# Layer 0's latent tiles as one, one and two instead of one and three, with new numbers of loop slots per unit

## The chip, the cores and the metric

The kernel runs on one core of one Trainium2 chip. The metric is the device time of one execution in microseconds (us). The kernel before takes 4186.02 us, the median of 3 runs (4184.7 to 4189.01).

## The reference, cut to what matters

Five tiles of 128 tokens (one prompt tile, four latent tiles) pass through two layers. Layer 0 is a mixer (chunked GLA heads beside pooling groups), layer 1 windowed attention; after either comes an output projection and then PEER, a layer of 16384 experts of which each token reads 128 (8 heads, 16 each):

```python
qh = (x @ w_q).reshape(T, PEER_HEADS, 2, PEER_HALF)
s = jnp.einsum('thcd,hcnd->thcn', qh, keys)
...                                   # top 16 of each half, top 16 of the pair sums
act = jax.nn.gelu(jnp.einsum('thkd,td->thk', u[eb], xb))
return jnp.einsum('thk,thkd->td', (gb * act).astype(xb.dtype), v[eb])
```

Everything is float32. For one tile and one of its 128 experts a row of u and of v (8 KB together) is fetched for each of the 128 tokens: 1.05 MB. There are 5 tiles, 2 layers and 128 experts, so 1280 such fetches.

## The kernel before, in words

**Two programs in one.** The first is the sequence of stages (norm, projection, GLA, pooling, output and norm, queries, selection, attention) on TensorE, VectorE and ScalarE. The second is the expert loop of class `Experts`, called the loop here. It is cut into 1280 slots, one for each fetch. For a slot GpSimd issues an indirect DMA into one of 8 ring buffers (L1889), VectorE makes the dot product of the u rows with the tile's hidden rows (L1906), ScalarE makes the weight (L1929, L1932) and either a diagonal matrix for TensorE (L1935), which adds the v rows (L1946), or nothing, and VectorE adds them (L1921). GpSimd's queue holds nothing but the fetches, in order, each waiting for its ring buffer, and at the start of a tile for that tile's selection. After a tile's 128 slots VectorE ends the tile (L1959 to L1963): it adds the sums to x. That is called a turn here.

**What sets the order.** The slots are written in between the instructions of the stages. Every stage has a number of units and a triple (slots per unit, ring places that TensorE adds, slots written at the stage's start, its lead); `PE_6` gives TensorE six of the eight places and VectorE two, `PE_8` all eight, and `PE_0` stands for none but the first and the last slot of a tile. After unit u the loop is brought up to slot `base + int(u * rate)` on each engine (`Stage.tick`), and at the stage's end to `base + int(units * rate)` (`Stage.__exit__`). `bg.allow(n)` sets the limit: no slot from n * 128 on is written until the call. A selection has 21 units by the count but ticks after 17 of them, so what belongs to the last 4 is written behind it. Every stage ends in a meeting of four engines (L153 to L168), and the tag of a stage is in its tiles' names.

**Layer 0.** The prompt tile goes first, without the loop. Then latent tile 1 alone goes through GLA, pooling, output, queries and selection as unit s0a while the loop works on the prompt tile's slots; latent tiles 2, 3 and 4 go through the same five stages together as unit s0b (their selections one by one). Output and queries stream their weights for each unit anew: `w_out` in 4 chunks, `peer_wq` in 16, the keys once, on SyncE's queue. Then come the modulation of layer 1 (`mod1`), `bg.finish(2)`, which runs the loop up to slot 384 and ends that tile if the loop isn't past it, and a meeting. If the loop is past slot 384 by then, `finish` only brings it to at least slot 388, which is nothing where it is past that too.

**Layer 1.** The prompt and latent tiles 1 and 2 go together (unit j1), with two selections, `j1_select0` under the limit 640 and `j1_select1` under 768; then tile 2 of attention as s1b and tiles 3 and 4 as s1c. After the last selection the loop runs alone up to slot 1280.

The slot that the loop has reached at the end of each stage, by the arithmetic above:

| stage | units | lead | per unit | slot at the end |
|---|---|---|---|---|
| s0a_query | 16 | 2 | 1.0 | 65 |
| s0a_select | 21 | 3 | 0.8 | 84 |
| s0b_gla, three tiles | 24 | 4 | 2.0 | 136 |
| s0b_pool | 3 | 4 | 2.0 | 146 |
| s0b_out | 18 | 3 | 1.75 | 180 |
| s0b_query | 16 | 2 | 2.0 | 214 |
| s0b_select2, 3, 4 | 21 each | 3 | 1.5, 2.1, 2.1 | 248, 295, 342 |
| mod1 | 12 | 3 | 2.5 | 375 |
| finish(2) | | | | 384 |
| j1_norm | 3 | 5 | 3.0 | 398 |
| j1_query | 16 | 2 | 1.0 | 582 |
| j1_select0, j1_select1 | 21 each | 3 | 2.0, 2.1 | 627, 674 |
| s1b_query, s1b_select | 16, 21 | 2, 3 | 1.15, 2.1 | 796, 843 |
| s1c_out, s1c_query | 12, 16 | 3, 2 | 1.9, 1.15 | 943, 963 |
| s1c_select3, s1c_select4 | 21 each | 3 | 2.0, 2.1 | 1008, 1055 |

## Time and profile before

| | us |
|---|---|
| median of 3 runs | 4186.02 |
| the profiled execution's own time | 4198.27 |
| its span in the trace | 4196.5 |
| TensorE busy | 2963.8 (71%) |
| VectorE busy | 3050.2 (73%) |
| ScalarE busy | 1414.7 (34%) |
| GpSimd busy | 1608.1 (38%) |

The profiled execution's time is 1.77 us over its span, and 12.25 us over the median. The DMA engines moved 1521.91 MB, a mean of 363 GB/s. The expert loop starts at 391 us, the last selection ends at 3615.5 us, and from there on only the loop runs. A stage's limits are read from the drains of its closing meeting; the windows shown further down are cut at these limits, one for each stage, and give for each engine the busy time with the number of instructions in brackets.

### The profile page before, as it was taken

To read this page: it belongs to the slowest core of one execution; us is meant where nothing else is said; L and a number is where in the kernel's file an instruction comes from. 1 tells how busy PE (TensorE), PEld (TensorE's weight loads), DVE (VectorE), ACT (ScalarE), POOL (GpSimd) and SP (SyncE) were. 2 spreads that over 40 slices of the span, in tenths; PEclk is the share of its full clock that TensorE was granted. 3 is DMA by queue.
4 is the path that set the end of the run, shared out by engine and by line. 5 is a ranking of instruction groups with operands and counts; after the bars stand their busy time and mean duration, and the time that the engine had idled before them with its cause. 6 is when DMAs were issued, how large, how long until landed. Compare 5 with 4: busy or idle time off the path is not lost.

```text
span 4196.5 us, 32629 instructions
## 1 busy us (share of the span) xinstructions
PE 2963.8 (71%) x9247; PEld 1533.7 (37%) x9247; DVE 3050.2 (73%) x6149; ACT 1414.7 (34%) x4109; POOL 1608.1 (38%) x1311
## 2 busy tenths in 40 slices
PE   5699756875877744857768776776877687665666
PEld 1365442444522311423446323444354543222222
DVE  0405769878897846697878876878787898666666
ACT  1212423532233312235522332432454233322222
POOL 0000332434544424344443443434433454454554
PEclk7798887987999976877879987878988899888888
DMA  7243897889998999899999999999999999999998
GB/s 305 110 156 114 311 407 288 332 339 362 417 397 360 396 407 390 339 391 407 374 383 390 417 374 365 364 379 417 395 372 391 414 406 380 423 420 409 415 421 369
DMA packets 222322, 1521.91 MB, mean 363 GB/s; under 512 B 29757, under 2 KB 33537, under 8 KB 48822
## 3 DMA queue, kind: packets, MB, share of 16 engines
q0 software_dynamic: 187200, 1370.25, 80.8%
q1 hardware_dynamic: 34942, 149.58, 9.0%
q8 instruction: 74, 1.21, 0.1%
q14 instruction: 106, 0.87, 0.1%
HBM read 1516.49 MB, written 3.24 MB: 362 GB/s over the span
## 4 chain that ended last, share of the span: by engine, by line
DMA 31%; PE 29%; DVE 24%; issue 7%; ACT 4%; POOL 2%; DVEq 1%; SPq 1%; PEldq 1%; PEld 0%; POOLq 0%; ACTq 0%
DMA core_ring<-in_l_uv,core_experts 27%; PE sum_rows L1946 7%; DVE core_ring L1906 7%; DVE core_yv L1921 5%; PE sum_rows L2213 2%; POOL core_ring L1889 2%; PE j_in_ps L471 2%; PE s1b_in_ps L471 1%; DMA s0a_h_w<-in_l_peer_wq 1%; PE s1c_query_pq L1679 1%; PE j_query_pq L1679 1%; DMA mod_w<-in_l_w_mod 1%; DVEq L158 1%; PE p_in_ps L471 1%; PE s0b_out_po L610 1%
## 5 line engine op out<-in xcount | busy, mean ns | idle before, releaser
L1889 POOL DMA_INDIRECT core_ring<-in_l_uv,core_experts x1280 | 1593.4, 1245 | 2233.3 <-PE sum_rows L1946 1104.6
L1946 PE MATMUL sum_rows<-core_ring,core_diag 128*128 128x512 f32 x3004 | 1646.0, 695 | 639.3 <-ACT core_diag L1935 506.5
L1906 DVE CUSTOM_DVE_ANT_0 core_ring<-core_ring,core_hc 128x1024 f32<-128x1024 f32 x1280 | 1552.2, 1223 | 659.7 <-DMA core_ring<-in_l_uv,core_experts 475.2
L1946 PEld LDWEIGHTS sum_rows<-core_ring,core_diag 128*128 128x128 f32 x3004 | 617.7, 219 | 1590.3 <-ACT core_diag L1935 848.9
L1929 ACT ACTIVATE core_wt<-core_wt 128x1 f32<-128x1 f32 x1280 | 256.5, 200 | 1681.3 <-DVE core_wt L1906 1589.4
L1921 DVE SCALAR_TENSOR_TENSOR core_yv<-core_ring,core_wt,core_yv 128x1024 f32<-128x1024 f32 x519 | 665.3, 1282 | 19.1 <-ACT core_wt L1932 18.6
L1932 ACT ACTIVATE core_wt<-core_wt,core_gates 128x1 f32<-128x1 f32 x1280 | 376.8, 294 | 41.5
L1935 ACT ACTIVATE core_diag<-core_ident,core_wt 128x128 f32<-128x128 f32 x751 | 301.5, 401 | 24.5
L2213 PE MATMUL sum_rows<-core_ring 128*128 128x416 f32 x320 | 117.6, 527 | 5.2 <-DVEq L158 4.1
L1929 ACT ACT_TABLE_LOAD x81 | 103.9, 1283 | 5.2 <-DVEq L158 3.8
L1906 DVE DVE_READ_ACCUMULATOR2_ANT core_wt<- 128x1 f32 x1280 | 105.6, 83 | 0.0
L1679 PE MATMUL s0b_query_pq<-s0b_h_hT,s0b_h_w 128*128 128x384 f32 x256 | 85.1, 497 | 5.4 <-DVEq L158 5.4
L2213 PEld LDWEIGHTS sum_rows<-core_ring 128*128 128x128 f32 x320 | 61.9, 196 | 57.0 <-issue 56.8
L2146 POOL DMA_DIRECT2D core_ring<-in_l_w_in x5 | 2.7, 535 | 205.4 <-PE sum_rows L2213 205.4
L357 PE MATMUL mod_pm<-mod_w,mod_c_silu 128*32 128x512 f32 x192 | 45.0, 944 | 38.6 <-DMA mod_w<-in_l_w_mod 38.6
L471 PE MATMUL j_in_ps<-j_in_w,j_atth_hT 128*128 128x384 f32 x192 | 64.8, 503 | 6.0 <-DMA j_in_w<-in_l_w_in 6.0
L1679 PE MATMUL j_query_pq<-s_att_pr,j_h_w 128*128 128x256 f32 x256 | 59.7, 393 | 8.8 <-DVEq L158 7.8
L1679 PEld LDWEIGHTS s0b_query_pq<-s0b_h_hT,s0b_h_w 128*128 128x128 f32 x256 | 49.7, 195 | 40.6 <-issue 8.0
L1679 PE MATMUL s1c_query_pq<-s1c_h_hT,s1c_h_w 128*128 128x256 f32 x256 | 57.4, 389 | 5.4 <-DVEq L158 5.4
L610 PE MATMUL s0b_out_po<-s0b_h_w,s0b_h_hT 128*128 128x256 f32 x192 | 49.4, 422 | 11.1 <-ACT s0b_h_hT L633 6.5
L1679 PEld LDWEIGHTS j_query_pq<-s_att_pr,j_h_w 128*128 128x128 f32 x256 | 49.7, 197 | 18.8 <-issue 8.2
L1598 ACT ACT_TABLE_LOAD x40 | 51.3, 1283 | 13.6 <-DVE s1c_attend_mx L1625 5.1
(772 smaller groups left out, 3060.2 us busy)
## 6 DMA issues: line engine op xcount, KB each, us to landing
mod_w<-in_l_w_mod SPq DMA_DIRECT2D x16, 2048.0 KB, 12.7
core_ring<-in_l_uv,core_experts POOLq DMA_INDIRECT x1280, 10.4
core_ring<-in_l_w_mod POOLq DMA_DIRECT2D x8, 2048.0 KB, 10.7
p_in_w<-in_l_w_in SPq DMA_DIRECT2D x5, 1664.0 KB, 9.1
core_ring<-in_l_w_in POOLq DMA_DIRECT2D x5, 1664.0 KB, 10.5
p_h_w<-in_l_peer_wq SPq DMA_DIRECT2D x16, 512.0 KB, 4.6
s0a_h_w<-in_l_peer_wq SPq DMA_DIRECT2D x16, 512.0 KB, 12.9
s0b_h_w<-in_l_peer_wq SPq DMA_DIRECT2D x16, 512.0 KB, 8.1
```

Of the source, the lines that this page charges most:

```text
L471: mm = nc.tensor.matmul(ps[:, i % 4, 0:chunk], hT[:, k, t * P:(t + 1) * P], w[:, n % 2, k, :], start=(k == 0), stop=(k == DK - 1))
L610: mm = nc.tensor.matmul(po[:, t % 2, n * CH:(n + 1) * CH], own(t)[:, k, :], w[n % w_slots][:, k * CH:(k + 1) * CH], start=(k == 0), stop=( ...
L1598: nc.scalar.activation(sc[:, n % 2, 0:w], sc[:, n % 2, 0:w], ACT.Exp, bias=mx[:, n % 2:n % 2 + 1], accum_out=den[:, t % 2, head:head + 1]) ...
L1679: mm = nc.tensor.matmul(pq[:, n % 2, 0:tok], queries.chunk(n)[:, k, :], hT[:, k, :], start=(k == 0), stop=(k == DK - 1))
L1889: nc.gpsimd.indirect_dma_start(self.ring[:, r, :], None, core.a[f"l{layer}_uv"], bass.IndirectOffsetOnAxis(ap=self.experts[:, t, n:n + 1], ...
L1906: nc.vector.tensor_tensor_reduce(self.ring[:, r, 0:D], self.ring[:, r, 0:D], self.hc[:], 1.0, 0.0, ALU.mult, ALU.add, self.wt[:, r:r + 1]) ...
L1921: x = nc.vector.scalar_tensor_tensor(self.yv[:], self.ring[:, r, D:], self.wt[:, r:r + 1], self.yv[:], ALU.mult, ALU.add)
L1929: nc.scalar.activation(self.wt[:, r:r + 1], self.wt[:, r:r + 1], ACT.Gelu_apprx_tanh).then_inc(self.gelu_done, 1)
L1932: nc.scalar.activation(self.wt[:, r:r + 1], self.wt[:, r:r + 1], ACT.Copy, scale=gate).then_inc(self.wt_done, 1)
L1935: nc.scalar.activation(self.diag[:, r, :], self.core.env["ident"][:], ACT.Copy, scale=self.wt[:, r:r + 1]).then_inc(self.diag_done, 1)
L1946: mm = nc.tensor.matmul(self.py[:, c * 512:(c + 1) * 512], self.diag[:, r, :], self.ring[:, r, D + c * 512:D + (c + 1) * 512], start=(at = ...
L2213: mm = nc.tensor.matmul(self.ps[:, i % 2 * 512:i % 2 * 512 + self.CH], self.hT[:, k, t * P:(t + 1) * P], w[:, k, :], start=(k == 0), stop= ...
```

## The change

Latent tiles 2, 3 and 4 no longer go as one unit. Tile 2 goes alone as unit s0b, in the way of tile 1: GLA and pooling for this tile, then `first_experts` with two weight buffers and the hidden rows of tile 3 as room for the transposed rows, under the limit 256. Tiles 3 and 4 follow as unit s0c, under the limit 384 and then as before. The numbers per unit are set anew.

```diff
--- before.py
+++ after.py
@@ -2357,9 +2357,10 @@
 PROMPT_RATES = {"norm": (3.0, PE_4, 5), "in": (2.0, PE_0, 4), "qk": (0.625, PE_4, 5), "attend": (2.25, PE_5, 3), "out": (1.5, PE_0, 4),
                 "query": (0.6, PE_0, 2), "select": (2.1, PE_8, 3)}
 FIRST_RATES = {"norm": (2.0, PE_4, 5), "decay": (2.0, PE_8, 0), "gla": (1.6, PE_6, 4), "pool": (2.0, PE_2, 4),
-               "out": (1.7, PE_0, 3), "query": (1.0, PE_0, 2), "select": (0.8, PE_8, 3)}
-REST_RATES = {"norm": (3.0, PE_4, 5), "gla": (2.0, PE_6, 4), "pool": (2.0, PE_2, 4), "out": (1.75, PE_0, 3), "query": (2.0, PE_0, 2),
-              "first select": (1.5, PE_8, 3), "select": (2.1, PE_8, 3)}
+               "out": (1.7, PE_0, 3), "query": (1.0, PE_0, 2), "select": (1.1, PE_8, 3)}
+SECOND_RATES = {"gla": (2.0, PE_6, 4), "pool": (2.0, PE_2, 4), "out": (1.9, PE_0, 3), "query": (1.15, PE_0, 2), "select": (1.8, PE_8, 3)}
+REST_RATES = {"gla": (2.0, PE_6, 4), "pool": (2.0, PE_2, 4), "out": (1.9, PE_0, 3), "query": (1.25, PE_0, 2),
+              "first select": (2.0, PE_8, 3), "select": (2.1, PE_8, 3)}
 LATENT_RATES = {"norm": (3.0, PE_4, 5), "in": (1.4, PE_0, 4), "qk": (1.125, PE_4, 5), "attend": (2.25, PE_5, 3), "out": (1.9, PE_0, 3),
                 "query": (1.15, PE_0, 2), "first select": (2.0, PE_8, 3), "select": (2.1, PE_8, 3)}
 
@@ -2408,8 +2409,11 @@
             layer0_mix(core, "s0a", latents, [0], pr, la, st, constants, (BAND_FIRST, BAND_AFTER), FIRST_RATES)
             first_experts(core, "s0a", first, 0, FIRST_RATES, None, 2, env["h"][:, others[0], :])
             bg.allow(2)
-            layer0_mix(core, "s0b", latents, [1, 2, 3], pr, la, st, constants, (BAND_AFTER, BAND_BEFORE), REST_RATES)
-        other_experts(core, "s0b", latents[1:], 0, 1, REST_RATES)
+            layer0_mix(core, "s0b", latents, [1], pr, la, st, constants, (BAND_AFTER, BAND_BEFORE), SECOND_RATES)
+            first_experts(core, "s0b", latents[1], 0, SECOND_RATES, None, 2, env["h"][:, latents[2], :])
+            bg.allow(3)
+            layer0_mix(core, "s0c", latents, [2, 3], pr, la, st, constants, (BAND_AFTER, BAND_BEFORE), REST_RATES)
+        other_experts(core, "s0c", latents[2:], 0, 2, REST_RATES)
         with Stage(core, "mod1_c") as m:
             modulation_stage(core, 1, "mod1", m.sb("silu", [P, DK, 32])[:], early.MOD_CHUNKS, [1, 4], 2, (2.5, PE_0, 3))
         with Stage(core, "s1_att") as m:
```
The slots at the ends of the stages are now:

| stage | units | lead | per unit | slot at the end |
|---|---|---|---|---|
| s0a_select | 21 | 3 | 1.1 | 91 |
| s0b_gla, one tile | 8 | 4 | 2.0 | 111 |
| s0b_pool | 1 | 4 | 2.0 | 117 |
| s0b_out | 6 | 3 | 1.9 | 131 |
| s0b_query | 16 | 2 | 1.15 | 151 |
| s0b_select | 21 | 3 | 1.8 | 191 |
| s0c_gla, two tiles | 16 | 4 | 2.0 | 227 |
| s0c_pool | 2 | 4 | 2.0 | 235 |
| s0c_out | 12 | 3 | 1.9 | 260 |
| s0c_query | 16 | 2 | 1.25 | 282 |
| s0c_select3, s0c_select4 | 21 each | 3 | 2.0, 2.1 | 327, 374 |
| mod1 | 12 | 3 | 2.5 | 407 |
| finish(2) | | | | 407 (writes nothing) |
| j1_norm | 3 | 5 | 3.0 | 421 |
| j1_query | 16 | 2 | 1.0 | 605 |
| j1_select0, j1_select1 | 21 each | 3 | 2.0, 2.1 | 640 (the limit), 687 |
| s1c_select4 | 21 | 3 | 2.1 | 1068 |

**SyncE's queue.** These rows are the loads of the output and query stages of unit s0b before; `h_w` is the weights' buffer, `room` holds the queries and the keys.

```order
L568 DMA s0b_h_w<-in_l_w_out 128x2048
L574 DMA s0bq_room<-mods 3x1024
L568 DMA s0b_h_w<-in_l_w_out 128x2048 x3
L519 DMA s0bq_room<-in_l_peer_keys 128x2048
L520 DMA s0bq_room<-in_k_count 128x32
L508 DMA s0b_h_w<-in_l_peer_wq 128x1024 x8
L166 UNCONDITIONAL_BRANCH
L171 ISA x16
L1666 UNCONDITIONAL_BRANCH
L508 DMA s0b_h_w<-in_l_peer_wq 128x1024 x8
```

And of the changed kernel, first unit s0b, then unit s0c:

```order
L568 DMA s0b_h_w<-in_l_w_out 128x2048
L574 DMA s0bq_room<-mods 3x1024
L568 DMA s0b_h_w<-in_l_w_out 128x2048 x3
L508 DMA s0b_h_w<-in_l_peer_wq 128x1024 x4
L519 DMA s0bq_room<-in_l_peer_keys 128x2048
L520 DMA s0bq_room<-in_k_count 128x32
L166 UNCONDITIONAL_BRANCH
L171 ISA x14
L1666 UNCONDITIONAL_BRANCH
L508 DMA s0b_h_w<-in_l_peer_wq 128x1024 x12
```

```order
L568 DMA s0c_h_w<-in_l_w_out 128x2048
L574 DMA s0cq_room<-mods 3x1024
L568 DMA s0c_h_w<-in_l_w_out 128x2048 x3
L519 DMA s0cq_room<-in_l_peer_keys 128x2048
L520 DMA s0cq_room<-in_k_count 128x32
L508 DMA s0c_h_w<-in_l_peer_wq 128x1024 x8
L166 UNCONDITIONAL_BRANCH
L171 ISA x16
L1666 UNCONDITIONAL_BRANCH
L508 DMA s0c_h_w<-in_l_peer_wq 128x1024 x8
```

`w_out`, the keys and the 16 chunks of `peer_wq` are loaded twice; with two buffers 4 query chunks go in the output stage and 12 in the query stage, with four buffers 8 and 8. The pooling constants (1.5 MB, ahead of each unit's GLA) are loaded once more too.

**VectorE around finish(2).** These rows stand ahead of the meeting before layer 1's norm (L156 is the meeting, L1906 the dot product, L1899 takes the next tile's hidden rows):

```order
L1921 SCALAR_TENSOR_TENSOR core_yv<-core_ring,core_wt,core_yv 128x1024
L1959 TENSOR_TENSOR core_yv<-core_yv,sum_rows 128x1024
L1961 TENSOR_TENSOR core_yv<-core_yv,core_g 128x1024
L1963 TENSOR_TENSOR core_x<-core_x,core_yv 128x1024
L156 UNCONDITIONAL_BRANCH
L2020 UNCONDITIONAL_BRANCH
L1899 COPY core_hc<-core_h 128x1024
```

In the changed kernel, from the last sums of `mod1` on (L320):

```order
L320 TENSOR_TENSOR mod_m<-mod_m,mod_ps 2x512 x2
L2020 UNCONDITIONAL_BRANCH
L156 UNCONDITIONAL_BRANCH
L2020 UNCONDITIONAL_BRANCH
L1906 ISA core_ring,core_wt<-core_ring,core_hc 128x1024
L1906 ISA core_wt 128x1
L1921 SCALAR_TENSOR_TENSOR core_yv<-core_ring,core_wt,core_yv 128x1024
```

The slots 375 to 383 and the end of the tile (L1959 to L1963) no longer stand between the modulation and the meeting; they stand in `mod1`, and the loop crosses the meeting in the middle of a tile.

**VectorE at the end of j1_select0.** Before, from the last wide reduction of the selection (L1808) on:

```order
L1808 TENSOR_REDUCE j_select_ef<-j_select_rest 128x128
L1906 ISA core_ring,core_wt<-core_ring,core_hc 128x1024
L1906 ISA core_wt 128x1
L1906 ISA core_ring,core_wt<-core_ring,core_hc 128x1024
L1906 ISA core_wt 128x1
L1810 SCALAR_TENSOR_TENSOR core_experts<-j_select_ef 128x128
L1813 TENSOR_REDUCE j_select_gs<-j_select_ts 128x8
L1814 RECIPROCAL j_select_gs<-j_select_gs 128x8
L1816 TENSOR_TENSOR core_gates<-j_select_ts,j_select_gs 128x128
L2020 UNCONDITIONAL_BRANCH
L1906 ISA core_ring,core_wt<-core_ring,core_hc 128x1024
L1906 ISA core_wt 128x1
```

After the change:

```order
L1808 TENSOR_REDUCE j_select_ef<-j_select_rest 128x128
L1810 SCALAR_TENSOR_TENSOR core_experts<-j_select_ef 128x128
L1813 TENSOR_REDUCE j_select_gs<-j_select_ts 128x8
L1814 RECIPROCAL j_select_gs<-j_select_gs 128x8
L1816 TENSOR_TENSOR core_gates<-j_select_ts,j_select_gs 128x128
L2020 UNCONDITIONAL_BRANCH x2
L1899 COPY core_hc<-core_h 128x1024
L1906 ISA core_ring,core_wt<-core_ring,core_hc 128x1024
L1906 ISA core_wt 128x1
L1906 ISA core_ring,core_wt<-core_ring,core_hc 128x1024
```

Before, ten slots stand behind L1808, two of them ahead of the four small operations that close the selection and eight behind them. After it none does, since the loop has reached the limit of 640 slots; the next one is the first slot of the tile that this selection chooses experts for.

## Rows read from the trace of the kernel before

**Rows 1.** The page: DMA queue of the gathers; the chain that ended last.
```profile
q0 software_dynamic: 187200, 1370.25, 80.8%
...
DMA 31%; PE 29%; DVE 24%; issue 7%; ACT 4%; POOL 2%; DVEq 1%; SPq 1%; PEldq 1%; PEld 0%; POOLq 0%; ACTq 0%
```

**Rows 2.** Windows, one per stage from s0a_select to j1_norm; the first row names the columns.
```profile
core 0: us, PE busy (x) PEld busy (x) DVE busy (x) ACT busy (x) POOL busy (x), PEclk, DMA share, GB/s
633.30:704.10 70.80, 46.66 (x96) 19.28 (x96) 69.14 (x258) 19.55 (x59) 21.61 (x18) 0.77 0.80 308
704.40:888.90 184.50, 146.25 (x696) 73.24 (x696) 164.26 (x280) 89.95 (x201) 64.69 (x53) 0.91 0.81 303
888.90:915.30 26.40, 19.89 (x104) 13.94 (x104) 20.76 (x29) 8.92 (x27) 12.52 (x10) 0.89 0.87 343
915.30:1038.80 123.50, 69.82 (x256) 53.64 (x256) 95.22 (x119) 30.67 (x86) 51.27 (x35) 0.73 0.95 377
1038.80:1133.50 94.70, 85.11 (x256) 49.71 (x256) 81.67 (x102) 23.06 (x84) 51.47 (x35) 0.95 1.01 408
1133.50:1222.40 88.90, 67.59 (x156) 29.39 (x156) 86.50 (x288) 33.04 (x104) 42.87 (x33) 0.93 0.98 396
1222.40:1355.10 132.70, 93.89 (x216) 38.15 (x216) 105.52 (x317) 44.70 (x143) 56.00 (x49) 0.92 0.90 372
1355.10:1478.50 123.40, 94.39 (x220) 39.14 (x220) 100.06 (x312) 45.10 (x144) 53.85 (x47) 0.96 0.99 399
1478.80:1633.30 154.50, 62.27 (x228) 13.87 (x228) 87.13 (x117) 25.63 (x82) 57.91 (x34) 0.65 0.97 395
1633.30:1663.10 29.80, 15.43 (x24) 5.27 (x24) 20.49 (x26) 7.38 (x26) 12.79 (x11) 0.79 1.00 400
1663.10:1712.90 49.80, 31.82 (x60) 13.89 (x60) 31.37 (x43) 21.26 (x48) 11.56 (x11) 0.64 0.62 244
```

**Rows 3.** Windows of other stages of the same kinds, and of the closing stretch.
```profile
438.40:504.20 65.80, 48.04 (x228) 23.89 (x228) 52.11 (x89) 27.73 (x62) 17.47 (x17) 0.87 0.87 329
519.50:573.90 54.40, 32.56 (x96) 21.43 (x96) 36.00 (x46) 14.84 (x36) 18.80 (x14) 0.72 0.98 400
573.90:633.30 59.40, 34.52 (x256) 32.05 (x256) 43.32 (x54) 11.75 (x52) 20.57 (x18) 0.95 1.02 417
2259.30:2371.40 112.10, 88.99 (x200) 38.32 (x200) 99.97 (x310) 42.92 (x137) 55.93 (x45) 0.93 0.99 394
2371.40:2501.60 130.20, 97.08 (x216) 39.86 (x216) 105.29 (x317) 44.71 (x143) 55.84 (x47) 0.91 0.93 380
2832.10:2895.20 63.10, 35.49 (x256) 33.67 (x256) 48.39 (x60) 12.80 (x56) 25.66 (x20) 0.85 1.02 417
2895.20:3013.80 118.60, 93.10 (x208) 38.81 (x208) 102.60 (x314) 44.70 (x143) 57.59 (x48) 0.93 1.01 417
3229.90:3316.20 86.30, 50.11 (x180) 36.15 (x180) 67.89 (x86) 23.22 (x64) 36.24 (x25) 0.76 1.02 419
3316.20:3376.50 60.30, 57.44 (x256) 49.99 (x256) 48.00 (x60) 14.30 (x56) 23.43 (x20) 0.97 1.01 411
3376.50:3487.40 110.90, 87.88 (x200) 35.84 (x200) 99.73 (x310) 42.92 (x137) 56.33 (x45) 0.94 0.99 407
3487.40:3615.50 128.10, 96.04 (x216) 39.98 (x216) 104.94 (x317) 44.71 (x143) 54.78 (x47) 0.91 0.95 387
3615.80:4196.50 580.70, 361.63 (x576) 127.37 (x576) 385.35 (x541) 169.31 (x594) 276.96 (x220) 0.82 0.99 408
```

**Rows 4.** The page's groups of instructions: the two VectorE operations of a slot.
```profile
L1906 DVE CUSTOM_DVE_ANT_0 core_ring<-core_ring,core_hc 128x1024 f32<-128x1024 f32 x1280 | 1552.2, 1223 | 659.7 <-DMA core_ring<-in_l_uv,core_experts 475.2
...
L1921 DVE SCALAR_TENSOR_TENSOR core_yv<-core_ring,core_wt,core_yv 128x1024 f32<-128x1024 f32 x519 | 665.3, 1282 | 19.1 <-ACT core_wt L1932 18.6
```

**Rows 5.** DMA issues between 704 and 1663 us: the weights of unit s0b.
```profile
s0b_h_w<-in_l_peer_wq SPq DMA_DIRECT2D x16, 512.0 KB, 8.1
...
s0b_h_w<-in_l_w_out SPq DMA_DIRECT2D x4, 1024.0 KB, 17.0
```

## The prediction

> **What bounds the kernel now.** I read the page first: the queue of the gathers alone takes 80.8% of the sixteen DMA engines' time, and the chain that ended last is led by its landings, 27% [rows 1]. The second view is one window per stage. In the closing stretch, where nothing but the loop runs, 225 slots (1055 to 1280) take 580.7 us at a DMA share of 0.99: 2.58 us a slot [rows 3]. That is the pace of the DMA engines, and the coin of this prediction: a slot that the loop does earlier takes 2.58 us from the end, and a stage that loads weights beside the loop pays in the same coin. In the stages from s0a_query on the share is 0.90 to 1.02 nearly everywhere; idle are s0a_select (0.80, VectorE busy 69.14 of 70.8 us), s0b_gla (0.81, VectorE 164.26 of 184.5 us) and j1_norm (0.62) [rows 2]. So only the first of these can be filled by writing more slots into it.
>
> A third thing to see is the price of a turn. Four selections of 47 slots with the same rate: j1_select1 and s1c_select4 hold a turn and take 130.2 and 128.1 us at a share of 0.93 and 0.95; s1b_select and s0b_select4 hold none and take 118.6 and 123.4 us [rows 2, 3]. The difference of the means, 8.2 us, is idle DMA time behind a turn.
>
> **The change part by part**, in us against the profiled execution, slots from the two tables.
>
> s0a_select goes from 19 to 26 slots. All of them are summed by TensorE there, so VectorE, which ends this stage, gets 7 dot products of 1.22 us [rows 4]: +8.5. At the loop's pace it would be 18.1, the upper bound; the lower is 6.8, as VectorE has 1.7 us free.
>
> GLA was 184.5 us for three tiles and 52 slots. The nearest row for one tile is s0a_gla, 65.8 us with 16 slots [rows 3]; 4 slots more at 1.22 + 1.28 / 4 (VectorE adds two of eight, [rows 4]) make 72.0. Two tiles are 72.0 + (184.5 - 8.2 - 72.0) / 2 = 124.2, with the turn at slot 128 taken out, since it moves to s0b_query. Together 196.2: +11.7. Bounds +2.4 (the 4 slots free) and +21.9 (4 at 2.58, and the turn no saving).
>
> Pooling was 26.4 us for 10 slots [rows 2]; 14 slots at the same 2.64 us are 37.0: +10.6 (at the loop's pace 4 slots are 10.3, so the ends lie close).
>
> The output stage: one tile with 14 slots is s0a_out, 54.4 us with 13, plus one slot, 57.0; two tiles with 25 slots are s1c_out, 86.3 us [rows 3]. Together 143.3 against 123.5 [rows 2]: +19.8. The turn at 256 now lies in it; weight loads can fill its gap, so between 0 and 8.2, and I take half, 4.1. Sum +23.9.
>
> The queries: one tile with 20 slots is s0a_query, 59.4 us with 18, plus two slots, 64.6 (s1b_query, with the same 20 slots, took 63.1); two tiles with 22 slots are s1c_query, 60.3 us with 20, plus two, 65.5 [rows 3]. Together 130.1 against 94.7 [rows 2]: +35.4, and half of a turn for slot 128: +39.5. This is the largest term, and it is the second reading of the weights: the old stage did 34 slots with one pass over `peer_wq`, the new ones 42 with two.
>
> What is read again is 12288 KB of the two weights [rows 5] and 2588 KB of keys, rows and pooling constants (shapes of the queue's rows), 15.2 MB. s0a_query moved 417 GB/s at a share of 1.02 [rows 3]; at this rate it is 36.5 us if no idle time takes any of it.
>
> The selections: 88.9 + 132.7 + 123.4 = 345.0 us for 128 slots [rows 2]. After: 40 slots at the pace of s1b_select (118.6 / 47 = 2.52), 100.8; 45 slots as s1c_select3, 110.9; 47 as the mean without a turn, 121.0 [rows 3]. s1c_select3 moved 110.9 us x 407 GB/s = 45.1 MB, two slots less than it used, so 5 us of it had been fetched ahead, and I add them: 337.7, -7.3. The lower bound is -12.3. VectorE doesn't end s0b_select: of its 86.50 us in s0b_select2, 34 dot products are 41.6, so the selection is 44.9, and with 40 slots it is 93.9, under 100.8.
>
> mod1 keeps its 33 slots and gets the turn at 384: half of one, +4.1.
>
> finish(2), 29.8 us for 9 slots and the end of the tile at a share of 1.00 [rows 2], goes but for the meeting: -29.5. What is late next is j1_norm. Its 14 slots went with 11 gathers issued, since the meeting had found the ring full [rows 2]; now the ring is empty at the meeting: 3 slots less two that its idle share can still take up to 7.7 us, I take 6.0. Bounds 0 and 7.7.
>
> Layer 1 runs as before with the loop 23 slots ahead, until j1_select0 meets the limit of 640: 35 slots instead of 45 there. The two selections of j1 lose 10 slots, -25.8. In return GpSimd has no fetch to issue until the selection is complete: the last reduction, four small operations, then a fetch that lands from an idle queue. I price it as a second turn, +8.2 (bounds 0 and 16.4): -17.6.
>
> The closing stretch has 212 slots instead of 225: -33.5.
>
> Sum: 8.5 + 11.7 + 10.6 + 23.9 + 39.5 - 7.3 + 4.1 - 29.5 + 6.0 - 17.6 - 33.5 = +16.4. The profiled execution took 4198.27 us, 12.25 over the median of the runs; a difference of this size carries over, so 4186.0 + 16.4 = 4202.4. In short: 36.5 us of loads, of which 20 find DMA time that was idle, in s0a_select and behind turns.
>
> **A rule of the skill.** In s0a_query 12 chunks of weights came on SyncE's queue beside GpSimd's gathers, and 18 slots took 59.4 us, 3.30 each instead of 2.58, at a share of 1.02 [rows 3]. The Trainium skill says it so (DMA: Bandwidth & Descriptors, "Issuing engines are not separate DMA queues"): DMAs of whatever engine run on the same 16 DMA engines and interleave. It speaks against this change, and read strictly it gives the first rival below; the trace agrees where the share is 1.02, and leaves room where it is 0.80. The skill's HBM Reference (Specifications) gives some 358 GB/s a core; by that the estimate for 15.2 MB would be 42.5 us, but the row has 417 GB/s, and the measurement decides.
>
> **The rivals.** First, full price: the reloads cost 36.5 us and no idle time is reclaimed, because what s0a_select takes up is lost again in front of the limit at 640 and in the additional start and end of a GLA stage. For it: GLA at 0.81, which the change doesn't touch and splits into two prologues [rows 2]. Against it: the selection's turn is surely gone. 4222.5.
>
> Second, the other side, faster: every turn that the change moves hides. The turns at 128, 256 and 384 move from stages without loads into s0b_query, s0c_out and mod1, which have weights to fetch whatever the ring does. If the loads fill the gap whole, and likewise the wait at 640 costs nothing since the selection would have to end anyway, all low bounds hold together: 8.5 + 2.4 + 10.6 + 19.8 + 35.4 - 12.3 + 0 - 29.5 + 0 - 25.8 - 33.5 = -24.4, so 4161.6. It decides for faster once a moved turn costs under 1 us in its new stage and GLA's two parts stay under 190 us together. Against it: mod1 at 0.97 and s0c_out's model at 1.02 have no slack, so a gap of 8 us there has nothing to be filled with but what the stage loads anyway [rows 2, 3].
>
> Third, the wait at 640 is dear: the fetch queue stands from the last fetch of the old tile until a landing, and the usual turn follows at once, each at 8.2 plus the lost cover of about 10 us: +26 to +28 in all, 4213.
>
> Fourth, the change does nothing that can be told: the gain of 13 slots and of finish (63 us) and the price of the split cancel closer than I have it. Within 0.2% of the median, 8.4 us, is about what a measurement of this kernel can tell from no change.
>
> **How the numbers follow.** The forecast (4194 to 4211) has 0.45, full price 0.20, dear wait 0.07, cancelling 0.14, faster 0.14. Of the forecast's own part some 0.06 lies inside 0.2%. Faster by over 0.2%: 0.15; within: 0.21; slower: 0.64. The range of 8 in 10 reaches down half of the way to the second rival and up past the first: 4177 to 4227; the forecast's own is 4194 to 4211.
>
> **What would show it.** In the windows of the changed kernel: s0b_query near 65 us and s0c_query near 66 at a share of 1.0 with 20 and 22 slots; s0b_out 57, s0c_out 86 to 94; s0a_select near 79 with VectorE over 0.95; the two GLA stages 72 and 124; no stretch of its own for finish; j1_select0 near 90 with an idle DMA gap at its end; the closing stretch 547. The bytes moved go from 1521.91 to about 1537 MB. The forecast is wrong if the four output and query stages stay under 250 us together, or if the closing stretch is not shorter by 33 us.

## The result

The changed kernel takes 4202.2 us, the median of 5 runs (4194.54 to 4210.25); the kernel before took 4186.02 us (4180.56 to 4189.01) beside it. The ratio is 1.0041, with a 95% interval from 1.0027 to 1.0055: slower by 0.27 to 0.55%. A second measurement on another chip gave 1.0031 [1.0017, 1.0046]. The forecast was 4202 us, with a range from 4177 to 4227.

**The profile after.** The profiled execution took 4194.54 us, the lowest of its five, while that of before lay 12.25 us over its median. So the two traces alone differ by -3.8 us where the medians differ by +16.2, and a sum over stages must be read with a second trace of the changed kernel beside it (4219.41 us, the highest of its ten). The page's rows that answer to [rows 1]:

```profile
q0 software_dynamic: 187200, 1370.25, 80.6%
q1 hardware_dynamic: 38932, 164.81, 9.9%
...
DMA 31%; PE 27%; DVE 25%; issue 8%; ACT 3%; POOL 2%; DVEq 1%; SPq 1%; PEldq 1%; PEld 0%; POOLq 0%; ACTq 0%
```

The gathers are the same bytes; SyncE's queue carries 15.2 MB more than the 149.58 MB and 9.0% of before. The two shares together are 90.5% of 4192.7 us, 3794 us of DMA time, against 89.8% of 4196.5 us, 3768 us; in the second trace 90.2% of 4217.6 us, 3804 us. So the DMA engines work 26 and 36 us longer and stand idle 30 and 15 us less (398 and 413 us instead of 428). Each share is printed to 0.1%, so each of these times is good to some 4 us. The mean, 22 us of idle time taken up, is near the forecast's 20 (of 36.5 us of loads).

Windows of the changed kernel, one per stage, with the columns of [rows 2]: s0a_select; GLA, pooling, output, queries and selection of s0b; the same of s0c with its two selections; mod1; the meeting in finish's place; j1_norm; j1_select0 and j1_select1; the closing stretch.

```profile
629.30:707.90 78.60, 55.23 (x124) 21.34 (x124) 77.16 (x272) 25.84 (x80) 30.60 (x25) 0.87 0.90 350
708.20:772.00 63.80, 52.05 (x244) 25.98 (x244) 57.80 (x98) 31.07 (x73) 25.36 (x22) 0.97 0.99 391
772.00:789.20 17.20, 10.72 (x44) 6.64 (x44) 11.24 (x16) 5.74 (x17) 6.28 (x5) 0.80 0.77 299
789.20:845.00 55.80, 32.64 (x100) 21.47 (x100) 35.31 (x47) 16.14 (x40) 18.63 (x13) 0.73 0.93 373
845.00:914.20 69.20, 41.33 (x260) 36.38 (x260) 51.40 (x63) 13.26 (x56) 24.38 (x21) 0.83 0.94 383
914.20:1014.80 100.60, 78.43 (x180) 33.97 (x180) 93.53 (x300) 38.42 (x122) 51.16 (x41) 0.92 1.01 415
1015.10:1141.50 126.40, 105.28 (x472) 52.42 (x472) 108.98 (x187) 60.27 (x137) 40.71 (x37) 0.88 0.89 342
1141.50:1164.10 22.60, 16.66 (x72) 10.42 (x72) 15.32 (x22) 7.21 (x22) 7.93 (x7) 0.87 0.78 287
1164.10:1258.20 94.10, 51.74 (x180) 36.58 (x180) 70.42 (x89) 23.91 (x66) 34.99 (x24) 0.74 0.97 389
1258.20:1321.10 62.90, 56.22 (x256) 49.06 (x256) 52.93 (x66) 15.86 (x60) 31.87 (x23) 0.96 0.98 402
1321.10:1433.20 112.10, 88.19 (x200) 37.90 (x200) 99.83 (x310) 42.92 (x137) 53.83 (x45) 0.92 1.01 416
1433.20:1554.70 121.50, 93.22 (x220) 38.62 (x220) 100.15 (x312) 45.11 (x144) 54.41 (x47) 0.97 0.99 404
1555.00:1710.50 155.50, 64.14 (x236) 15.15 (x236) 88.43 (x119) 26.43 (x84) 64.50 (x34) 0.66 0.97 396
1710.50:1714.90 4.40, 0.00 (x0) 0.00 (x0) 0.00 (x0) 0.00 (x0) 0.00 (x0) 0.50 1.00 411
1714.90:1773.90 59.00, 35.38 (x64) 15.89 (x64) 33.58 (x44) 22.16 (x51) 14.34 (x12) 0.63 0.57 222
2322.70:2413.80 91.10, 69.78 (x160) 29.68 (x160) 87.52 (x290) 33.94 (x107) 38.70 (x30) 0.91 0.90 353
2413.80:2542.20 128.40, 95.81 (x216) 39.55 (x216) 105.03 (x317) 44.71 (x143) 60.95 (x52) 0.90 0.96 395
3647.90:4192.70 544.80, 336.52 (x544) 117.54 (x544) 363.18 (x510) 159.65 (x560) 258.47 (x207) 0.82 0.99 410
```

Beside the second trace, term by term, in us against the trace of before (worked out from unrounded limits, so a tenth can differ from the rows above):

| term | forecast | after | second trace |
|---|---|---|---|
| s0a_select | +8.5 | +7.8 | +7.8 |
| GLA | +11.7 | +5.7 | +11.9 |
| pooling | +10.6 | +13.4 | +14.8 |
| output | +23.9 | +26.3 | +29.6 |
| queries | +39.5 | +37.5 | +38.4 |
| three selections | -7.3 | -10.7 | -9.0 |
| mod1 | +4.1 | +0.9 | +0.9 |
| finish | -29.5 | -25.4 | -25.5 |
| j1_norm | +6.0 | +9.2 | +15.0 |
| j1's selections | -17.6 | -22.8 | -24.2 |
| closing stretch | -33.5 | -35.9 | -35.0 |
| sum | +16.4 | +6.0 | +24.7 |

The mean of the two sums is +15.4. That it lies so near the medians' +16.2 says little, since there is only one trace of the kernel before. Stages that the change doesn't touch differ between the first two traces by some -10 us together; I take that for the spread of single executions (the ten times of the changed kernel on the second chip span 26.6 us).

### The profile page after: what moved, and what is told of

Read it like the earlier page. It is cut to its first block, busy times and chain, and to the rows that moved or that the text cites. A ratio compares the mean times of both kernels' runs of the same rounds, so it can differ in the third digit from the quotient of the medians.

```text
span 4192.7 us, 33299 instructions
## 1 busy us (share of the span) xinstructions
PE 2957.0 (71%) x9507; PEld 1564.2 (37%) x9507; DVE 3050.0 (73%) x6153; ACT 1420.3 (34%) x4128; POOL 1609.9 (38%) x1311
## 3 DMA queue, kind: packets, MB, share of 16 engines
q8 instruction: 76, 1.25, 0.1%
## 4 chain that ended last, share of the span: by engine, by line
DMA 31%; PE 27%; DVE 25%; issue 8%; ACT 3%; POOL 2%; DVEq 1%; SPq 1%; PEldq 1%; PEld 0%; POOLq 0%; ACTq 0%
DMA core_ring<-in_l_uv,core_experts 25%; PE sum_rows L1946 7%; DVE core_ring L1906 7%; DVE core_yv L1921 5%; PE sum_rows L2213 2%; POOL core_ring L1889 2%; PE j_in_ps L471 2%; PE s1c_query_pq L1679 1%; DVEq L158 1%; PE j_query_pq L1679 1%; DMA mod_w<-in_l_w_mod 1%; PE s1b_in_ps L471 1%; PE p_in_ps L471 1%; PE p_query_pq L1679 1%; PE j_out_po L610 1%
## 5 line engine op out<-in xcount | busy, mean ns | idle before, releaser
L1946 PE MATMUL sum_rows<-core_ring,core_diag 128*128 128x512 f32 x2996 | 1625.4, 690 | 604.6 <-ACT core_diag L1935 462.2
L1906 DVE CUSTOM_DVE_ANT_0 core_ring<-core_ring,core_hc 128x1024 f32<-128x1024 f32 x1280 | 1549.8, 1223 | 662.4 <-DMA core_ring<-in_l_uv,core_experts 435.9
L1946 PEld LDWEIGHTS sum_rows<-core_ring,core_diag 128*128 128x128 f32 x2996 | 613.3, 218 | 1538.1 <-ACT core_diag L1935 798.5
L1921 DVE SCALAR_TENSOR_TENSOR core_yv<-core_ring,core_wt,core_yv 128x1024 f32<-128x1024 f32 x521 | 667.1, 1280 | 19.1 <-ACT core_wt L1932 18.8
L1929 ACT ACT_TABLE_LOAD x82 | 105.2, 1283 | 7.1 <-DVEq L158 5.7
L1906 DVE DVE_READ_ACCUMULATOR2_ANT core_wt<- 128x1 f32 x1280 | 104.6, 82 | 0.0
L471 PE MATMUL j_in_ps<-j_in_w,j_atth_hT 128*128 128x384 f32 x192 | 63.8, 496 | 9.6 <-DMA j_in_w<-in_l_w_in 9.6
L357 PE MATMUL mod_pm<-mod_w,mod_c_silu 128*32 128x512 f32 x192 | 40.0, 865 | 36.4 <-DMA mod_w<-in_l_w_mod 36.4
L1679 PEld LDWEIGHTS j_query_pq<-s_att_pr,j_h_w 128*128 128x128 f32 x256 | 49.2, 196 | 19.7 <-issue 8.2
L1679 PE MATMUL s0c_query_pq<-s0c_h_hT,s0c_h_w 128*128 128x256 f32 x256 | 56.2, 383 | 0.4 <-PEq L163 0.4
L1598 ACT ACT_TABLE_LOAD x40 | 51.3, 1283 | 15.1 <-DVE s1a_attend_mx L1625 4.4
L1679 PEld LDWEIGHTS s1c_query_pq<-s1c_h_hT,s1c_h_w 128*128 128x128 f32 x256 | 50.0, 196 | 13.0 <-issue 5.8
L1679 PE MATMUL s0a_query_pq<-core_h,s0a_h_w 128*128 128x128 f32 x256 | 39.0, 318 | 21.0 <-DMA s0a_h_w<-in_l_peer_wq 17.9
## 6 DMA issues: line engine op xcount, KB each, us to landing
mod_w<-in_l_w_mod SPq DMA_DIRECT2D x16, 2048.0 KB, 12.5
core_ring<-in_l_uv,core_experts POOLq DMA_INDIRECT x1280, 10.5
core_ring<-in_l_w_in POOLq DMA_DIRECT2D x5, 1664.0 KB, 10.7
s0a_h_w<-in_l_peer_wq SPq DMA_DIRECT2D x16, 512.0 KB, 12.5
```

The lines of the kernel that those rows point to most:

```text
L471: mm = nc.tensor.matmul(ps[:, i % 4, 0:chunk], hT[:, k, t * P:(t + 1) * P], w[:, n % 2, k, :], start=(k == 0), stop=(k == DK - 1))
L1598: nc.scalar.activation(sc[:, n % 2, 0:w], sc[:, n % 2, 0:w], ACT.Exp, bias=mx[:, n % 2:n % 2 + 1], accum_out=den[:, t % 2, head:head + 1]) ...
L1679: mm = nc.tensor.matmul(pq[:, n % 2, 0:tok], queries.chunk(n)[:, k, :], hT[:, k, :], start=(k == 0), stop=(k == DK - 1))
L1906: nc.vector.tensor_tensor_reduce(self.ring[:, r, 0:D], self.ring[:, r, 0:D], self.hc[:], 1.0, 0.0, ALU.mult, ALU.add, self.wt[:, r:r + 1]) ...
L1921: x = nc.vector.scalar_tensor_tensor(self.yv[:], self.ring[:, r, D:], self.wt[:, r:r + 1], self.yv[:], ALU.mult, ALU.add)
L1929: nc.scalar.activation(self.wt[:, r:r + 1], self.wt[:, r:r + 1], ACT.Gelu_apprx_tanh).then_inc(self.gelu_done, 1)
```

## The experiments

Four questions: what a second pass over the weights costs, what the moved turns cost, what the late limit and the lost finish cost, and what the numbers of slots do without the split. Each kernel ran beside the kernel before.

**Fewer bytes in s0b's weight stages.** From the changed kernel:

```diff
...
+                few = DK * CH // queries.part
+                sp.dma_start(w[n % w_slots][:, 0:few], w_dram[n][:, 0:few]).then_inc(w_in[n % w_slots], 16)
...
+            queries.part = 8 if tag == "s0b" else 1
```

The load of `peer_wq` is cut in the same way, and the matmuls take eight times the same eighth.

> The changed kernel, but unit s0b loads only an eighth of each chunk of w_out and peer_wq and multiplies by that eighth eight times, so that every instruction stands where it stood and 11.0 MB less is read (its output and queries are therefore not those of the reference). If the price of the change is the second reading at the pace of the DMA engines, 11.0 MB at 0.41 MB per us are 27 us: about 4175 us, 0.9974 of the kernel before, and s0b_out and s0b_query together go from 125 to under 105 us. If the price is the splitting itself (two starts and ends of each stage, small units) and the reads are hidden, it stays at 4202 us, 1.004.

Measured: 4195.83 us against 4192.4, ratio 1.0008 [0.9992, 1.0025]. The windows of s0b_out and s0b_query in it:

```profile
796.90:852.30 55.40, 34.05 (x100) 21.69 (x100) 35.30 (x47) 16.14 (x40) 18.24 (x13) 0.72 0.78 298
852.30:909.00 56.70, 37.78 (x260) 33.47 (x260) 50.66 (x63) 13.30 (x56) 31.82 (x21) 0.89 0.87 343
```

The query stage falls by 12.5 us (69.2 to 56.7). The output stage falls by only 0.4 against the first trace of the changed kernel (55.8), while its DMA share drops from 0.93 to 0.78. That trace had the quickest of five such stages, though: those that have it unchanged took 55.8 to 60.0 us (58.8 in the second trace), so the bytes are worth 0.4 to 4.6 us there. An output stage of one tile with 14 slots has some 55 us of work that the bytes don't set.

The two stages take 112.1 us together, not under 105, and the ratio lies between the two that were expected. By the ratios 11.0 MB are worth 10 to 14 us of the kernel's time (1.0041 or 1.0031 less 1.0008), half of what 417 GB/s would make of them, 26 us. The intervals leave anything from about 0 to 23 us. Without these bytes the kernel can't be told from the kernel before.

**The same reads added to the kernel before.** Every chunk of `w_out` and `peer_wq` in unit s0b is loaded a second time, into a buffer that nothing reads:

```diff
...
+        self.again(sp, self.dram[n])
...
+                queries.again(sp, w_dram[n][:, 0:DK * P])
+                queries.again(sp, w_dram[n][:, DK * P:])
...
```

> The kernel before, whose output and query stages of unit s0b load every chunk of w_out and peer_wq a second time into memory that nothing reads: 12.6 MB more, no stage split, no slot moved. If the reads are the price, 12.6 MB at 0.41 MB per us are 31 us: about 4217 us, 1.0073 of before. SyncE waits for the landing of the load before the last ahead of each, which could add some us. If the reads are hidden beside the stages' other waits, it stays within 5 us of before, 1.000 to 1.001.

Measured: 4213.69 us, 1.0052 [1.0032, 1.0073]. Windows of s0b_out and s0b_query, against 123.5 and 94.7 us in [rows 2]:

```profile
908.00:1041.80 133.80, 74.09 (x256) 55.51 (x256) 95.38 (x119) 30.66 (x86) 50.50 (x35) 0.73 0.98 395
1041.80:1148.80 107.00, 87.94 (x256) 50.12 (x256) 82.03 (x102) 23.06 (x84) 45.74 (x35) 0.93 1.02 419
```

12.6 MB cost 10.3 + 12.3 = 22.6 us there and 22 us in all (0.0052 of 4192), where 417 GB/s makes it 30. The interval, 13 to 31 us, doesn't exclude 30, and what SyncE's waits for the landings add isn't told apart. With little idle DMA time left (share 0.98 and 1.02) bytes are paid at three quarters of their price here; in a stage with a pace of its own, such as s0b_out above, at much less.

**The split alone.** The changed kernel with the slots of the first selections such that 342 and 375 slots are reached where the kernel before reached them:

```diff
-               "out": (1.7, PE_0, 3), "query": (1.0, PE_0, 2), "select": (1.1, PE_8, 3)}
+               "out": (1.7, PE_0, 3), "query": (1.0, PE_0, 2), "select": (0.8, PE_8, 3)}
```

and 1.3 for 1.8 and 2.0 in the two selections behind it.

> The changed kernel with fewer slots per unit in three selections (s0a_select 0.8, s0b_select 1.3, the first of s0c 1.3), so that the loop stands at 342 at the end of s0c and at 375 at the end of mod1, as in the kernel before, and finish(2) is back: the split without the slots that came with it. If the change is reads at full price, less what its additional slots find of idle DMA time, this one pays the whole 36.5 us: 4222 us, 1.0087 of before. If where the slots stand is of no consequence, because a slot costs the DMA engines the same anywhere, it takes as long as the changed kernel: 4202 us, 1.004.

Measured: 4212.27 us, 1.0050 [1.0032, 1.0068]. The windows of s0b_query, s0c_out and s0c_query:

```profile
842.00:905.30 63.30, 41.74 (x264) 36.67 (x264) 49.16 (x62) 13.93 (x58) 29.05 (x20) 0.84 1.02 418
1129.50:1216.50 87.00, 48.37 (x176) 35.28 (x176) 69.10 (x87) 23.23 (x64) 37.53 (x26) 0.76 1.02 419
1216.50:1290.80 74.30, 62.63 (x264) 51.99 (x264) 54.29 (x68) 16.23 (x62) 25.45 (x22) 0.91 0.95 381
```

The stages that the split touches sum to +18.8 us against the trace of before: queries +42.9, pooling +11.4, output +23.6, the selections with 107 slots instead of 128 -58.8, and little from GLA (-1.6), mod1 (+3.7) and finish (-2.4). So the split alone is the loss, +21 us by the ratio (13 to 29 by its interval), and that is not the full price of 36.5: some 15 us of the reloads found idle DMA time although s0a_select kept its 19 slots. The new slots of the changed kernel bring some 4 to 8 us back, which the intervals (around 1.0041, 1.0031 and 1.0050) don't tell from nothing.

**The first selection back to 19 slots** in the changed kernel, the limit of 640 as it is: the edit of the diff above alone.

> The changed kernel with one number back: the first selection stage takes 19 slots as in the kernel before, all else as changed; the limit of 640 turns stays, so the 7 slots go to the first joint selections and not to finish. Theory A (a slot costs what its stage pays for it): -7.8 us in the first selection, +7 x 2.3 = +16 us in the first joint selection, sum +8, against the changed kernel; so 1.006 of the kernel before. Theory B (what counts is the number of slots in all): no difference, 1.004.

Measured: 4200.6 us, 1.0042 [1.0027, 1.0056]: the time of the changed kernel, not 8 us more. That is the number of theory B, but no proof of it: the selection takes 7.9 us less (70.7) and j1_select0 13.6 more (104.7), and the two turns at 128 and 256 move as well. These two kernels show what a turn costs by its place. In the changed kernel the turn at slot 128 is the first thing in s0b_query. Windows of 6 us there, then three of the operations from 850 us on (start, duration, operation, idle time before it and what ended it):

```profile
845.00:851.00 6.00, 0.82 (x1) 0.50 (x2) 5.58 (x7) 0.99 (x4) 0.94 (x1) 0.67 0.98 397
851.00:857.00 6.00, 6.00 (x33) 4.26 (x32) 3.55 (x6) 0.66 (x3) 2.16 (x3) 0.77 0.19 41
857.00:863.00 6.00, 4.22 (x38) 4.03 (x37) 6.00 (x9) 2.10 (x9) 4.16 (x3) 1.00 1.01 419
```

```profile
850.18 3.77 PE L1946 MATMUL sum_rows<-core_ring,core_diag 128*128 128x512 f32 x4 [5.31 <-DVE core_x L1963]
...
854.23 0.94 POOL L1889 DMA_INDIRECT core_ring<-in_l_uv,core_experts  x1 [8.15 <-PE sum_rows L1946]
...
855.77 14.58 SPq L508 DMA_DIRECT2D s0b_h_w<-in_l_peer_wq  x6
```

In its queue TensorE has the loop's matmul (L1946) ahead of the queries'. The first waits 5.31 us for the end of the tile (L1963), and the queries' matmuls start behind it, at 853.75 us. So no weight buffer comes free and SyncE issues no chunk until 855.77 us; GpSimd has no free ring place until 854.23. The DMA engines have nothing to do: a share of 0.19, 4.9 us lost. With 19 slots in s0a_select the same turn comes 18 to 24 us into the query stage (63.6 us there instead of 69.2), while chunks are under way. The window of 6 us with the turn in it:

```profile
858.00:864.00 6.00, 0.00 (x0) 0.00 (x0) 4.76 (x5) 0.29 (x1) 0.00 (x0) 0.70 1.02 418
```

TensorE and GpSimd stand still there too, and the DMA engines lose nothing. The loads are behind in this stage: TensorE waits 10.9 us for chunks (us in total, times, longest):

```profile
PE s0b_query_pq L1679 <- DMA s0b_h_w<-in_l_peer_wq: 10.9, 5, 3.0
```

The turn at 256 falls across the end of s0c_out in the changed kernel:

```profile
1246.00:1252.00 6.00, 4.54 (x12) 2.57 (x11) 4.57 (x8) 2.58 (x8) 0.94 (x1) 0.69 0.88 366
1252.00:1258.00 6.00, 3.63 (x4) 1.18 (x4) 3.03 (x3) 0.00 (x0) 0.00 (x0) 0.60 0.53 179
1258.00:1264.00 6.00, 5.60 (x23) 4.71 (x23) 5.53 (x7) 1.76 (x7) 4.03 (x4) 0.83 0.64 227
```

This is 0.12 + 0.47 + 0.36 of 6 us, 5.7 us lost. The turn at 384 lies in mod1, at 1630 us, and the share stays at 0.98 or more from 1608 to 1656 us: nothing lost. In the kernel before, the turn at 256 stood in a selection:

```profile
1258.00:1264.00 6.00, 0.00 (x0) 0.00 (x0) 5.93 (x29) 1.08 (x4) 0.00 (x0) 0.50 0.07 30
1264.00:1270.00 6.00, 3.65 (x5) 1.59 (x6) 5.79 (x13) 0.90 (x3) 0.00 (x0) 0.50 0.00 0
```

with 11.6 us lost in these two windows alone, and 2.8 more in the next (share 0.54).

With 19 slots the turn at 256 comes 21 us into s0c_query, while chunks are still being issued (until 1283 us), and yet DMA time is lost:

```profile
1258.00:1264.00 6.00, 1.96 (x6) 0.63 (x4) 5.65 (x7) 1.27 (x5) 1.23 (x1) 0.94 1.01 421
1264.00:1270.00 6.00, 5.63 (x9) 3.20 (x10) 1.06 (x2) 0.00 (x0) 1.27 (x2) 0.50 0.51 208
```

From 1264 to 1288 us it is 3.7 us. In the split alone the turn comes 51 us into s0c_query, behind the last chunk's issue, and 4.8 us are lost in the 30 us from 1270 on. TensorE waits for no chunk in s0c_query in either trace. So the middle of a stage that streams weights doesn't by itself make a turn free. It was free where TensorE had been waiting for weights (10.9 us in s0b_query with 19 slots, 36.4 in mod1). That is read from these traces; no experiment varied it.

In these two kernels s0c_out with s0c_query take 161.3 us, against 157.0 in the changed kernel; s0b_out with s0b_query take 123.3 and 120.2, against 125.0 to 129.1 in the five traces that have the turn at the stage's start. One pair gains what the other loses, which with the selections leaves nothing that the interval can tell. My expectation had counted the selections alone.

**No wait at 640.** In layer 1's joint unit the output stage gets 1.5 slots a unit instead of 2.0 and the queries 0.75 instead of 1.0, so that j1_select0 has its 45 slots again and ends at the limit without meeting it earlier:

> The changed kernel with ten slots fewer ahead of j1_select0 (output stage 1.5 instead of 2.0 a unit, queries 0.75 instead of 1.0), so that the loop does not run into the limit of 640 before the selection is complete; the slots at the ends of j1_select0 and j1_select1 are the same 640 and 687. If the wait at the limit costs what I took for it, a turn's 8 us of idle DMA time, it is 8 us under the changed kernel. If the ten slots cost the same wherever they are and the wait lies beside the turn that comes anyway, the two are within 3 us.

Measured: 4212.91 us, 1.0052 [1.0038, 1.0067], against 1.0031 [1.0017, 1.0046] of the changed kernel on the same chip. The window of j1_select0:

```profile
2325.30:2436.60 111.30, 87.79 (x200) 35.97 (x200) 99.81 (x310) 42.93 (x137) 57.25 (x45) 0.94 0.98 396
```

Ten slots fewer save 9.2 us in j1_out (87.3 for 96.5) and 2.8 in j1_query, and cost 20.2 in j1_select0, which is back at its old 112; j1_select1 is 1.9 shorter. Against the changed kernel on the same chip the medians say +10.5 us, which is neither -8 nor within 3, though the two intervals overlap. This didn't isolate the wait: with fewer slots the DMA share fell to 0.86 in j1_out and 0.93 in j1_query (0.92 and 1.01 in the changed kernel), and that idle time went with it. The changed kernel, with its wait at the limit, wasn't the dearer of the two.

**The constants of attention issued later.** SyncE issues the seven loads of L1354 to L1360 behind the norm rows, not ahead of the meeting:

```diff
...
+            if "late" in env:
+                env.pop("late")(sp)
...
```

> The changed kernel, but SyncE issues the seven loads of attention constants (L1354 to L1360) behind the load of the norm's rows in j1_norm instead of ahead of the meeting. My theory of what took back 7 us of the gain at finish(2): the meeting now waits for SyncE's seven issues, some 4 us, and the norm's rows land behind 1.1 MB of constants, some 5 to 8 us. It expects 4193 us, 1.0017 of before, with the meeting under 1 us and j1_norm near 52 us. The rival, that j1_norm is longer because the ring isn't full at the meeting, expects the meeting's 4 us at most: 4198 us, 1.003, with j1_norm still near 59 us.

> The kernel with the attention constants behind the norm's rows once more, now beside the changed kernel on one chip. Its trace showed the meeting and j1_norm 14 us shorter than in the changed kernel, yet its ratio to before was the same 1.004. If the 14 us count, it is 1.0007 to 1.002, some 8 to 14 us under the changed kernel of the same call. If the DMA engines fetch the same bytes in the same total time whatever waits there, since the meeting's 4 us had them at a share of 1.01, it is within 4 us of the changed kernel.

Measured: 4210.45 us, 1.0040 [1.0025, 1.0056], and 4204.74 us, 1.0035 [1.0021, 1.0050]. The meeting goes from 4.4 to 0.9 us and j1_norm to 48.8 and 50.9, as expected for these two stages; in the total there is nothing of it. The first trace had these two stages 14 us shorter and the medians no gain; the second run repeated both.

**The changed kernel once more**, for a second trace and ratio:

> The changed kernel itself, on the same chip as the three kernels that follow, as what they are compared with. 1.004 of the kernel before, about 16 us more, as measured.

Measured: 4202.38 us, 1.0031 [1.0017, 1.0046].

What the two traces and this experiment say together of j1_norm. The rows of tile j_norm_rows, first in the changed kernel, then in its second trace, then in the kernel without the wait at 640 (the L393 row is the issue, the L366 row the first use, behind the counts the first and the last start in us):

```profile
L366 PE MATMUL j_norm_ps<-j_norm_rows,core_ident x7: 1056/1056/1217, 1729.3 to 1734.6; 4*128 4x512 f32 x7
L393 SPq DMA_DIRECT2D j_norm_rows<-mods x2: 254/256/258, 1715.1 to 1715.4; - x2
```

```profile
L366 PE MATMUL j_norm_ps<-j_norm_rows,core_ident x3: 1056/1056/1215, 1753.1 to 1755.0; 4*128 4x512 f32 x3
L393 SPq DMA_DIRECT2D j_norm_rows<-mods x2: 254/256/259, 1731.3 to 1731.6; - x2
```

```profile
L366 PE MATMUL j_norm_ps<-j_norm_rows,core_ident x7: 1056/1056/1217, 1744.5 to 1749.8; 4*128 4x512 f32 x7
L393 SPq DMA_DIRECT2D j_norm_rows<-mods x2: 254/256/257, 1738.4 to 1738.8; - x2
```

Three executions issue the same rows behind the same seven loads and use them after 14.2, 21.8 and 6.1 us; the kernels with fewer bytes and with 19 slots, with the same queue, after 7.4 and 8.4; before it was 6.9 (1663.3 to 1670.2), with the loads 26 us ahead. The ring is no part of this: up to the meeting GpSimd had issued 413 gathers and VectorE made 407 dot products in all of these but the one with 19 slots (406 and 400), six ahead each time; before it was eight (392 and 384). SyncE's part around the meeting in the changed kernel:

```profile
1711.42 0.33 SPq L1354 DMA_DIRECT2D s_att_gain<-in_l_q_norm  x1
...
1714.23 0.44 SPq L1360 DMA_DIRECT2D s_att_sink<-in_l_sink  x1
1715.08 0.57 SPq L393 DMA_DIRECT2D j_norm_rows<-mods  x2
```

The seven issues, 3.3 us, are the 4.4 us that stay in finish's place: the slots of finish had covered them. Why the same two small loads are used after 6 us in one execution and after 22 in another isn't settled.

**Other slots, no split.** Since the split alone is the slower part, the kernel before with the rest of the idea:

```diff
-FIRST_RATES = {"norm": (2.0, PE_4, 5), "decay": (2.0, PE_8, 0), "gla": (1.6, PE_6, 4), "pool": (2.0, PE_2, 4),
-               "out": (1.7, PE_0, 3), "query": (1.0, PE_0, 2), "select": (0.8, PE_8, 3)}
+FIRST_RATES = {"norm": (2.0, PE_4, 5), "decay": (2.0, PE_8, 0), "gla": (2.0, PE_6, 4), "pool": (2.0, PE_2, 4),
+               "out": (1.7, PE_0, 3), "query": (1.0, PE_0, 2), "select": (1.1, PE_8, 3)}
```

and 1.9 for 2.0 in the rest queries, so that 383 slots are written when `finish` comes.

> The kernel before, without any split, with the slots that VectorE can take in stages where the DMA engines idle: s0a_gla 2.0 instead of 1.6 a unit, s0a_select 1.1 instead of 0.8, and the queries of s0b 1.9 instead of 2.0. The loop stands at 383 instead of 375 before finish(2). By my theory this is the part of the change that pays: 8 slots at 2.58 us leave the end, 20.6 us, against 4.6 us for three slots in GLA and 8.5 for seven in the selection, less 5.2 for two in the queries: 12 to 13 us under the kernel before, 0.997. If the place of a slot is of no consequence it is 1.000.

> The kernel before with other slots and no split (first GLA stage 4 loop slots a unit more in all, first selection 26 instead of 19, rest queries 32 instead of 34): a second look, on another chip, at the kernel that came out at 4167.85 us and 0.9952 of the kernel before. If the gain belongs to the slots (finish 10.1 instead of 29.8 us with 1 slot instead of 9), the ratio is 0.995 again, 0.9935 to 0.9970. If it was a matter of that chip or of chance, it is 0.998 or above.

Measured: 4167.85 us, 0.9952 [0.9934, 0.9970], and on another chip 4170.69 us, 0.9962 [0.9948, 0.9976]. It is faster than both kernels. The first trace's windows of s0a_gla, s0a_select, s0b_select3 and finish:

```profile
434.00:502.40 68.40, 51.81 (x240) 25.41 (x240) 57.58 (x98) 30.81 (x73) 26.61 (x22) 0.91 0.92 361
630.50:710.00 79.50, 56.21 (x124) 24.23 (x124) 77.21 (x272) 25.83 (x80) 29.42 (x25) 0.87 0.87 342
1221.60:1346.40 124.80, 96.18 (x216) 39.39 (x216) 105.46 (x317) 44.71 (x143) 58.45 (x50) 0.92 0.97 400
1627.50:1637.60 10.10, 3.71 (x4) 1.17 (x4) 7.38 (x7) 1.39 (x5) 3.80 (x3) 0.67 0.92 370
```

Against [rows 2, 3], four slots more in s0a_gla cost 2.6 us and seven in s0a_select 8.7; two fewer in the rest queries save 4.3 (90.4 us), and finish with one slot instead of nine saves 19.7. The sum is -12.7. The expectation took these slots from the closing stretch, but that stays at 580.6 us; it is finish that pays.

There is a second gain, which the expectation doesn't have: s0b_select3 takes 124.8 us instead of 132.7 (125.9 in the second trace) and s0b_select2 2.5 less. The turn at 256 stands 16 us into s0b_select3 now instead of 43, and 4.9 us of DMA time are lost at it (1239 to 1251 us) instead of 14.4. With it the sum is -23.1, for -20 and -16 by the medians. The bytes are those of before, so the gain is DMA time that stood idle (the second trace: shares of 81.4 and 9.1% of 4169.9 us, which leaves 396 us idle instead of 428).

One of these numbers alone, the first selection at 1.1:

> The kernel before with one number changed, no split: the first selection stage takes 26 loop slots instead of 19, and the units behind it so many fewer just ahead of the meeting. Theory A (a slot run in finish, where TensorE has nothing beside it, costs 29.8 us / 9 = 3.3 us, and 8.2 us / 7 = 1.2 us in the first selection): +8 in the selection, -20 to -25 in finish, 0 to +6 given back in the normalisation behind it, where SyncE's loads then come late; sum -6 to -12 us, ratio 0.9970 to 0.9985. Theory B (slots move and cost the same wherever they run): 0, ratio 1.000.

Measured: 4176.33 us, 0.9980 [0.9968, 0.9992], so about -8 us (-13 to -3), inside what was expected: +7.8 in the selection and -17.0 in finish (12.8 us with two slots). But s0b_select3 is 8.1 us shorter here too (124.6), which theory A doesn't have, and with it these stages come to -17, twice what the medians show. The number came out; the account behind it isn't complete.

And the same numbers as in the faster kernel with a lead of 8 instead of 5 for layer 1's norms, six slots taken from the closing stretch:

> The kernel of the other slots (4167.85 us) with, in layer 1, the normalisation stages ahead of the limit by 8 slots instead of 5, by which some 6 slots move out of the closing stretch, where one costs 580.7 / 225 = 2.58 us, into layer 1's units, where they cost 1.2 to 2.4 us. If closing slots are paid in full: -4 to -8 us against that kernel, 0.993 to 0.994 of the kernel before. If the units pay as much: no difference, 0.995.

Measured: 4174.67 us, 0.9977 [0.9966, 0.9988]; not faster than without it, 0.9962 on the same chip, where 4 to 8 us less were expected if closing slots are paid in full. The closing stretch falls from 580.7 to 563.3 us, and the stages ahead of it take it back: s1b_norm goes from 36.3 to 42.3 us, j1_norm from 49.8 to 52.0, and the selections j1_select1 and s1c_select4 are 3 and 4 us longer. So 17.4 us saved at the end came back as 15.3 in these four stages. The slots went into norms that had idle DMA time (a share of 0.81 in s1b_norm and 0.56 in j1_norm without the edit), and that alone didn't make them cheap: idle time in a stage is no proof that slots can take it.

## Why the prediction was right, step by step

**The mechanism held in the main; that the number is right to 0.2 us is luck.** The sum of the terms was +16.4 us; the medians say +16.2 and, on the second chip, +13.0, each known to some 6 us either way. Single terms were off by up to 6.0 us in the first trace and 9.0 in the second (GLA, j1's selections, j1_norm), with both signs, and they cancel. The four output and query stages took 282.0 us, not under 250, and the closing stretch is 35.9 shorter, so neither sign of a wrong forecast came up. The DMA engines' time grew by 26 and 36 us, less than the loads' 36.5 or as much, and 30 and 15 us of idle time went.

**Where the idle time was found** is only in part where the forecast had it, in s0a_select and behind turns. A window's length times one less its share gives its idle DMA time. It fell from 14 to 8 us in s0a_select and from 16 to nothing in the selections of layer 0 behind it, as forecast. The largest part is GLA, from 35 to 15 us (0.81 before, 0.99 and 0.89 after; 0.93 and 0.91 in the split alone). The turn at 128 is 7.7 of that; for the rest the prediction has GLA's share as one that the change doesn't touch. Why GLA idles less in two parts isn't shown. On the other side queries and pooling idle 11 us more, j1_norm 6 and j1's selections 4. This is from one trace, but the second has 19 us in GLA and the split alone 15.

**The moved turns.** I took half of 8.2 us for each of the three, 12.3 in all, without a reason that tells one from another. The DMA time lost at them is 4.9, 5.7 and about 0, sum 10.6. The sum is near by luck, since the three differ so. The 8.2 itself is a mean of places that differ too: it came from four selections of 47 slots, and the fifth, s0b_select3 with 132.7 us, would make it 9.3. The second rival (the loads fill the gap whole) is right where the loads were behind (mod1, s0b_query with 19 slots). It is wrong at the boundary of a stage, where TensorE's wait holds full buffers, and in s0c_query, where TensorE never waits for weights; two of the three turns fell on such boundaries.

**Queries and output** came out at +37.5 and +26.3 for +39.5 and +23.9. The models of one and two tiles without a turn were close: 64.6 for 63.3 to 63.6 in s0b_query, 86.3 for 87.0 and 87.8 in s0c_out.

**GLA** came out at +5.7 and +11.9 for +11.7, by parts that were mis-sized: 63.8 and 69.7 us for 72.0 with one tile, 126.4 and 126.7 for 124.2 with two. In the split alone the two tiles take 119.6 us with the same 36 slots; why it is 7 us more in the changed kernel is open.

**The first rival (full price, no idle time taken)** falls by the result itself, since 4222.5 us would be 1.0087 and the interval ends at 1.0055. The experiments agree: 11.0 MB are worth 10 to 14 us and the split alone 21, not 26 and 36.5. Its reason, two starts of GLA, doesn't hold in the split alone, where the two GLA stages take 63.3 + 119.6 = 182.9 us for 56 slots, no more than the 184.5 for 52; in the changed kernel they take 190.2 and 196.4, with four slots more than before.

**The wait at 640** was priced as a second turn, 8.2 us; j1's selections show -22.8 and -24.2 against -17.6, so by the price of 2.58 us a slot it costs 2 to 3 us over the ten slots' 25.8. The idle DMA time of the two windows agrees: 14 us instead of 10. The third rival (26 to 28 us, 1.0065) lies above the interval.

**The step that failed is finish and j1_norm.** I wrote "goes but for the meeting", 0.3 us; 4.4 are left, since the meeting waits for SyncE's seven issues. For j1_norm I took 6.0 from a ring empty at the meeting. It wasn't empty: six gathers were ahead of the dot products there, for eight before, and the stage issued 12 and 11 gathers, not fewer than the 11 of before. The stage was +9.2 and +15.0 in the changed kernel's traces by the late norm rows, but +1.5, -0.7 and +1.5 in the kernels with fewer bytes, without the wait and with 19 slots, which run the same code there with the same six ahead. So the ring's price was small, and what is large is a wait for two small loads that varies. Moving the constants' loads took it away in the trace and not in the medians, which stays open.

## What to carry to other kernels

Where a background loop bounds the kernel by DMA time, price an edit in two lists: bytes added, which cost their price only where the DMA share is already near 1.0 (22 of 30 us here, and about half where it was lower), and idle DMA time, which is all that a slot written earlier can take. Splitting a unit that streams weights pays for the weights twice; here that was +21 us, where three changed numbers and no split gave -16 to -20. A turn, or any wait that stops TensorE, cost nothing here where TensorE had been waiting for weights, and 3.7 to 5.7 us of DMA time at a stage's start or end or where the weights were there in time; in a selection it cost 4.9 or 14.4, by its place. So look for such waits first, and place the turn by slots. And before removing a stretch of waiting, look for what another queue did behind it.

## What the runs showed of the hardware that was not expected

An output stage of one tile (s0b_out) took 55.4 us at a DMA share of 0.78 with an eighth of its weights' bytes, and 55.8 to 60.0 us at 0.93 to 0.87 with all of them. Gathers and weight loads together moved 418 and 419 GB/s for stretches of 63 to 107 us; gathers in selections moved 415 and 416 over 101 and 112 us. Two loads of 8 KB each, issued in 0.57 us behind seven others, were used after 6.1 to 21.8 us in five executions of the same order of instructions. The same turn in a selection lost 14.4 us of DMA time 43 us into the stage, and 4.9 us 16 us into it.
